# A transformer block pair on one core: the overflow blocks of the expert layer in another order on every engine

## The reference

```python
_, eidx = lax.top_k(scores + router_bias.astype(jnp.float32), TOP_K_EXPERTS)
...
def expert_block(args):
    e, toks, gs = args
    xb = t[toks]
    return swiglu(xb, w1[e], w3[e], w2[e]) * gs[:, None]
...
routed = jax.ops.segment_sum(out.reshape(rows, D), row_tok, num_segments=n_tok)
```

## Time and profile before

| what | us |
|---|---|
| median of 3 runs | 2405.52 |
| lowest and highest run | 2403.63, 2409.03 |
| the profiled execution, its own time | 2403.76 |
| its span, first to last instruction | 2402.0 |
| step 0 of the experts to the last | about 460 to 1053 |
| the three overflow blocks | about 1053 to 1098 |
| loading and adding up the rows | 1101 to 1154 |

### The profile page before, as it was taken

The page is one execution under the profiler, slowest core; times in us unless marked ns, Lnnn a source line. Parts: engine busy times, 40 slices in busy tenths (PEclk is TensorE's granted clock), DMA queues, the critical chain, the costliest instruction groups (busy, mean ns, idle before and its releaser), DMA issues.

```text
span 2402.0 us, 30744 instructions
## 1 busy us (share of the span) xinstructions
PE 2260.3 (94%) x10236; PEld 1761.8 (73%) x10236; DVE 1568.2 (65%) x2403; ACT 1198.4 (50%) x1774; POOL 237.7 (10%) x312
## 2 busy tenths in 40 slices
PE   7999999899999999992999999999999889999997
PEld 5776676778888888872666788888778557888885
DVE  7789766899999999986665643333452676433344
ACT  4433434588888888871335332233222673322333
POOL 0000000333323333320000000000020000000000
PEclk9999999999999999996999999999999899999999
DMA  8411243799999999986220222223222001322332
GB/s 332 169 62 62 88 158 125 267 367 395 381 390 401 388 387 388 378 309 282 100 77 1 79 97 96 96 96 106 97 88 97 27 14 66 114 96 96 105 102 82
DMA packets 97377, 424.09 MB, mean 177 GB/s; under 512 B 20305, under 2 KB 20561, under 8 KB 70496
## 3 DMA queue, kind: packets, MB, share of 16 engines
q1 hardware_dynamic: 77168, 386.86, 43.6%
q0 software_dynamic: 19648, 34.72, 3.8%
q10 hardware_dynamic: 432, 0.87, 0.1%
HBM read 421.81 MB, written 39.45 MB: 192 GB/s over the span
## 4 chain that ended last, share of the span: by engine, by line
PE 77%; DVE 8%; issue 5%; ACT 5%; DMA 3%; DVEq 2%; SPq 0%; POOLq 0%; POOL 0%; ACTq 0%
PE PS L298 22%; PE PS L300 21%; PE PS L299 21%; ACT wh L192 3%; PE PS L714 2%; PE PS L2006 2%; PE PS L736 2%; DMA YG<-expert_rows 1%; DVE wl L197 1%; PE PS L725 1%; DMA ada_wa<-wada 1%; PE PS L2031 1%; DVEq L1285 1%; DVE M L1282 1%; PE PS L1245 1%
## 5 line engine op out<-in xcount | busy, mean ns | idle before, releaser
L197 DVE TENSOR_TENSOR wl<-raw,wh 128x1024 fp32r<-128x1024 f32 x239 | 292.4, 1225 | 357.1 <-ACT wh L192 350.9
L298 PE MATMUL PS<-HTh,wh 128*128 128x512 f32 x1248 | 498.5, 399 | 6.3 <-ACT V L881 2.2
L300 PE MATMUL PS<-HTh,wl 128*128 128x512 f32 x1248 | 486.9, 390 | 0.0
L299 PE MATMUL PS<-HTl,wh 128*128 128x512 f32 x1248 | 486.9, 390 | 0.0
L197 DVE TENSOR_TENSOR wl<-eraw,wh 128x1024 fp32r<-128x1024 f32 x384 | 458.5, 1221 | 17.5 <-ACT wh L192 14.5
L192 ACT ACTIVATE wh<-raw 128x1024 fp32r<-128x1024 f32 x239 | 252.0, 1056 | 368.9 <-PE PS L300 344.5
L192 ACT ACTIVATE wh<-eraw 128x1024 fp32r<-128x1024 f32 x384 | 392.5, 1054 | 16.8 <-PE PS L300 14.7
L298 PEld LDWEIGHTS PS<-HTh,wh 128*128 128x128 f32 x1248 | 234.5, 188 | 72.3 <-issue 13.7
L299 PEld LDWEIGHTS PS<-HTl,wh 128*128 128x128 f32 x1248 | 234.7, 188 | 50.0 <-issue 3.4
L300 PEld LDWEIGHTS PS<-HTh,wl 128*128 128x128 f32 x1248 | 234.7, 188 | 49.6
L298 PE MATMUL PS<-wh,XTh 128*128 128x512 f32 x536 | 221.1, 413 | 2.7 <-DVE wl L2192 1.5
(11 more groups left out here) (416 smaller groups left out, 3432.2 us busy)
## 6 DMA issues: line engine op xcount, KB each, us to landing
eraw<-wstream SPq DMA_DIRECT2D x192, 1024.0 KB, 7.5
raw<-wstream SPq DMA_DIRECT2D x240, 512.0 KB, 3.3
YG<-expert_rows SPq DMA_DIRECT2D x16, 1024.0 KB, 15.8
ada_w<-wada SPq DMA_DIRECT2D x20, 512.0 KB, 5.6
eraw<-wexp SPq DMA_DIRECT2D x9, 1024.0 KB, 6.8
ada_wb<-wada SPq DMA_DIRECT2D x2, 2048.0 KB, 15.5
ada_l<-wada SPq DMA_DIRECT2D x8, 512.0 KB, 3.4
ada_g<-wada SPq DMA_DIRECT2D x2, 2048.0 KB, 10.4
```

Of the source, the lines that this page charges most:

```text
L197: nc.vector.tensor_tensor(wl[:, ci % RING, :], src, wh[:, ci % RING, :].bitcast(F32), ALU.subtract).then_inc(split_done, 1)
L298: nc.tensor.matmul(o, lh, rh, start=start, stop=False)
L299: nc.tensor.matmul(o, lh, rl, start=False, stop=False)
L300: return nc.tensor.matmul(o, ll, rh, start=False, stop=stop)
```

## The change

TensorE, ScalarE, VectorE. The rows of block p + 1 are turned ahead of chunks 2 and 3 of block p, and chunks 0 and 1 of block p + 1 go between chunks 3, the turned `HG` and 4 of block p; for block 0 they go into step 63, ahead of the down chunks of expert 63. `XTh`, `XTl`, `SG`, `HG`, `HHh`, `HHl` and bank 0 or 1 alternate by p mod 2. The four slots of `wh` and `wl` follow the new order (`more_at`). `YS` of block p is read out inside ScalarE's block p + 1 (`previous_y`), and at the end of the last block for that one.

GpSimd. Gate of p + 2 and gather of p + 3 stand behind the output copy of p; ahead of block 0's copy stand gate 1 and gather 2. There is a drain between the copy of `YIXC` and the output copy. In the last block GpSimd also waits for the gather of p + 3. SyncE waits for two more products ahead of the third pair of a block's chunks.

```diff
+            def more_at(p, c):
+
+                return c if p == 0 and c < 2 else 6 * p - 2 + c if c < 2 else 6 * p + c if c < 4 else 6 * p + 2 + c
+
+            def more_slot(p, c, i):
+
+                return (c - 2 if p == 0 and c < 2 and not isinstance(i, int) else more_at(p, c)) % RING
+
+            def more_turn(p, c, i):
+
+                at = -2 + c if p == 0 and c < 2 and not isinstance(i, int) else more_at(p, c)
+                return i * (6 * GROUP) + at
...
                 act.wait_ge(ov["xt"], i * GROUP + (p + 2))
-                if isinstance(i, int) and p == 0:
-                    act.wait_ge(chunk_used, up_end(E - 2))
-                nc.scalar.activation(XTh[:, 0, :], PS[:, 2:4, :].rearrange("p a b -> p (a b)"), ACT.Copy).then_inc(ov["xc"], 1)
+                if isinstance(i, int) and p < 2:
+                    act.wait_ge(chunk_used, up_end(E - 2 + p))
+                else:
+                    act.wait_ge(ov["used"], i * (6 * GROUP) + (6 * (p - 2) + 4 + ER))
+                nc.scalar.activation(XTh[:, p % 2, :], PS[:, 2:4, :].rearrange("p a b -> p (a b)"), ACT.Copy).then_inc(ov["xc"], 1)
...
+                nc.vector.tensor_tensor(XTl[:, p % 2, :], PS[:, 2:4, :].rearrange("p a b -> p (a b)"),
+                                        XTh[:, p % 2, :].bitcast(F32), ALU.subtract).then_inc(ov["xl"], 1)
...
+                if isinstance(i, int) and p == 0 and c < 4:
+                    act.wait_ge(chunk_used, EXPERT1 + c + 1)
+                else:
+                    act.wait_ge(ov["used"], more_turn(p, c, i) + (ER - RING + 1))
+                nc.scalar.activation(wh[:, more_slot(p, c, i), :], eraw[:, ER_PLACE[g % ER], :], ACT.Copy).then_inc(ov["high"], 1)
...
+                dve.wait_ge(ov["high"], more_turn(p, c, i) + 1)
+                nc.vector.tensor_tensor(wl[:, more_slot(p, c, i), :], eraw[:, ER_PLACE[g % ER], :],
+                                        wh[:, more_slot(p, c, i), :].bitcast(F32), ALU.subtract).then_inc(ov["split"], 1)
...
+            def more_product(pe, p, c, i=0):
+
+                pe.wait_ge(ov["split"], more_turn(p, c, i) + 1)
...
+                    if c < 4:
+                        r = slice((2 * c + kk) * P, (2 * c + kk) * P + P)
+                        mm = three_pass(PS[:, p % 2, :], XTh[:, p % 2, r], XTl[:, p % 2, r], wgh, wgl, c + kk == 0, c + kk == 4)
+                    else:
+                        r = slice((c - 4) * P, (c - 3) * P)
+                        mm = three_pass(PS[:, 6 + kk, :], HHh[:, p % 2, r], HHl[:, p % 2, r], wgh, wgl, c == 4, c == 5)
+                mm.then_inc(ov["used"], 1)
...
+            def after(eng, p, i):
+
+                return more[eng.engine] > i * GROUP + (p + 1)
+
+            def no_more(eng, p, i):
+
+                return more[eng.engine] <= i * GROUP + (p + 1)
...
+                    if n + 1 == E:
+                        with pe.If(more[pe.engine] > 0):
+                            pe.wait_ge(ov["xl"], 1)
+                            more_product(pe, 0, 0)
+                            more_product(pe, 0, 1)
...
+                    if n + 1 == E:
+                        with act.If(more[act.engine] > 0):
+                            more_high(act, 0, 0)
+                            more_high(act, 0, 1)
                     act_ht(act, n, i)
...
                     split(d0 + 1 + AHEAD, at)
                     if n + 1 == E:
                         with act.If(more[act.engine] > 0):
-                            for c in range(2):
-                                more_high(act, 0, c)
+                            more_high(act, 0, 2)
+                            more_high(act, 0, 3)
                     act_y(act, n, i)
...
+                        with dve.If(more[dve.engine] > 0):
+                            more_low(dve, 0, 0)
+                            more_low(dve, 0, 1)
                     dve_ht(dve, n, i)
...
                         with dve.If(more[dve.engine] > 0):
-                            for c in range(2):
-                                more_low(dve, 0, c)
+                            more_low(dve, 0, 2)
+                            more_low(dve, 0, 3)
...
-                        sp.wait_ge(ov["used"], i * (6 * GROUP) + (g + 2))
+                        sp.wait_ge(ov["used"], i * (6 * GROUP) + (g + (4 if c == 4 else 2)))
                         sp.dma_start(eraw[:, at:at + 2, :], wexp[e, c:c + 2].rearrange("c p n -> p c n")
                                      ).then_inc(expert_arrived[g % ER // 2], 16)
...
                 def block_(p, i):
                     y = 2 + p % 2
-                    more_gate(p + 1, i)
+                    if isinstance(i, int) and p == 0:
+                        more_gate(1, 0)
+                        more_gather(pool, 2, code_of(2, 0), 0)
                     pool.tensor_copy(YIXC[:, y:y + 1], YIX[:, bass.ds(code_of(p, i), 1)])
-                    more_gather(pool, p + 2, code_of(p + 2, i), i)
+                    pool.drain()
                     pool.wait_ge(ov["y"], i * GROUP + (p + 2))
                     pool.sem_inc(passed_pool, 1)
                     pool.indirect_dma_start(out=yrows, out_offset=bass.IndirectOffsetOnAxis(ap=YIXC[:, y:y + 1], axis=0),
...
                     pool.wait_ge(ov["rows"], i * (16 * GROUP) + 16 * (p + 3))
                     pool.sem_inc(passed_pool, 1)
+                    more_gate(p + 2, i)
+                    more_gather(pool, p + 3, code_of(p + 3, i), i)
+                    with pool.If(no_more(pool, p, i)):
+                        pool.wait_ge(ov["rows"], i * (16 * GROUP) + 16 * (p + 4))
+                        pool.sem_inc(passed_pool, 1)
```

The blocks of TensorE, ScalarE and VectorE:

```diff
+                    more_xt(pe, p + 1, i)
+                    more_product(pe, p, 2, i)
+                    more_product(pe, p, 3, i)
+                    with pe.If(after(pe, p, i)):
+                        pe.wait_ge(ov["xl"], i * GROUP + (p + 2))
+                        more_product(pe, p + 1, 0, i)
+                    pe.wait_ge(ov["hid"], i * GROUP + (p + 1))
+                    with pe.If(no_more(pe, p, i)):
+                        pe.sem_inc(ov["used"], 2)
+                    for f in range(2):
+                        mm = nc.tensor.transpose(PS[:, 4, f * P:(f + 1) * P], HG[:, p % 2, f * P:(f + 1) * P], const("ident"))
+                    mm.then_inc(ov["ht"], 1)
+                    with pe.If(after(pe, p, i)):
+                        more_product(pe, p + 1, 1, i)
+                    pe.wait_ge(ov["hl"], i * GROUP + (p + 1))
+                    pe.wait_ge(y_ready, E)
+                    pe.wait_ge(ov["y"], i * GROUP + (p + 1))
+                    more_product(pe, p, 4, i)
+                    more_product(pe, p, 5, i)
...
-                    for c in range(2, 6):
-                        more_high(act, p, c, i)
+                    more_xh(act, p + 1, i)
+                    if p or not isinstance(i, int):
+                        previous_y(p, i)
+                    with act.If(after(act, p, i)):
+                        more_high(act, p + 1, 0, i)
+                        more_high(act, p + 1, 1, i)
                     act.wait_ge(ov["used"], i * (6 * GROUP) + (6 * p + 4 + ER))
-                    nc.scalar.activation(SG[:, 0, :], PS[:, 0, 0:256], ACT.Silu).then_inc(ov["silu"], 1)
+                    nc.scalar.activation(SG[:, p % 2, :], PS[:, p % 2, 0:256], ACT.Silu).then_inc(ov["silu"], 1)
+                    with act.If(no_more(act, p, i)):
+                        act.sem_inc(ov["high"], 2)
+                    more_high(act, p, 4, i)
                     act.wait_ge(ov["ht"], i * GROUP + (p + 1))
-                    nc.scalar.activation(HHh[:, 0, :], PS[:, 4, 0:256], ACT.Copy).then_inc(ov["hc"], 1)
-                    more_xh(act, p + 1, i)
-                    with act.If(more[act.engine] > i * GROUP + (p + 1)):
-                        for c in range(2):
-                            more_high(act, p + 1, c, i)
-                    act.wait_ge(ov["used"], i * (6 * GROUP) + (6 * p + 6 + ER))
+                    nc.scalar.activation(HHh[:, p % 2, :], PS[:, 4, 0:256], ACT.Copy).then_inc(ov["hc"], 1)
+                    more_high(act, p, 5, i)
+                    with act.If(after(act, p, i)):
+                        more_high(act, p + 1, 2, i)
+                        more_high(act, p + 1, 3, i)
+                    with act.If(no_more(act, p, i)):
+                        previous_y(p + 1, i)
+
+                def previous_y(q, i):
+                    act.wait_ge(ov["used"], i * (6 * GROUP) + (6 * q + 2 + ER))
                     for s in range(2):
                         act.wait_ge(y_out[s], 16 * E // 2)
-                    act.wait_ge(ov["sent"], i * GROUP + (p + 1))
-                    nc.scalar.activation(YS[:, p % 2, :], PS[:, 6:8, :].rearrange("p a b -> p (a b)"), ACT.Copy).then_inc(ov["y"], 1)
+                    act.wait_ge(ov["sent"], i * GROUP + q)
```

(24 more changed lines are left out.)

38 lines of the change are left out of this document (5 added, 33 removed).

## The result

| | before | changed |
|---|---|---|
| median of 11 runs each | 2403.69 | 2411.03 |
| lowest and highest | 2396.15, 2409.03 | 2408.29, 2420.74 |
| the profiled execution, its own time | 2403.76 | 2408.29 |
| its span | 2402.0 | 2406.5 |

The ratio is 1.0041, with a 95% interval of 1.0028 to 1.0054: 6.7 to 13.0 us slower, 9.9 in the middle. The two medians alone are 7.3 apart, inside that interval. One execution of the changed kernel, of 4596.93, stands alone and is left out of the row of lowest and highest and of the ratio; without it the median would be 2410.85. The forecast was 2416, slower than before; the range of 2406 to 2424 holds the time.

The account below looks back on a forecast made before the run. The prediction took GpSimd seeing its last DMA land as the bound on the overflow stretch. Its steps moved that from 1098.2 to 1110.7, 12.5 us slower, so 2403.8 became 2416.3; own range 2410 to 2421, wider range 2406 to 2424.

Parts of the forecast that it names:

- Step (1): Step 63: two new products and splits stand ahead of the readout of expert 63, making it 4.7 us later.
- Step (2): Output copy 63: issued 2.0 us behind the readout, lands 5.1 later; its drain ends at 1069.9 instead of 1066.0.
- Step (3): Gather 2: issued at 1073.2, 5.2 us in flight; block 2's rows turned at 1078.4 instead of 1076.01.
- Steps (4) and (5): Block 2's rows to block 3's: 11.9 us; last block, turning to readout: 10.0 instead of 5.6, GpSimd deciding copy 2.
- Step (6): Tail: copy 2 lands, drain, then GpSimd waits for an absent block's gather; last landing 1110.7 instead of 1098.2.
- The signs: Traces expected if right, including drains of 3 to 6 us and TensorE idle 4 to 6 before block 2's turning.
- A drain doesn't wait for landings: GpSimd's drains: long ones end with landings only by chance; 4.4 us slower, 2408; chance 0.12.
- The overlap does its work: Overflow blocks: GpSimd's waits fall beside TensorE's work, gather 2 issued by 1068, idle 6.5 us filled; 2397.3; chance 0.06.
- The loads are heavier: DMA under weight loads: copy 63 lands 6.0 later, its drain lasts 4 longer, copy 0 takes 5.1; 2423; chance 0.12.

Follow-up runs that it names:

- early: tail with the first split of block 0 moved up into step 62, both products still ahead of the down products of expert 63; 2407.23, ratio 1.0020.
- tail: Changed kernel, but in the last block GpSimd neither issues nor waits for the absent block's gather, nor reads its gate; 2407.26, ratio 1.0026.
- compold: Old orders on TensorE, ScalarE and VectorE with the changed kernel's order on GpSimd; 2406.76, ratio 1.0015.
- poolold: Changed kernel's orders on TensorE, ScalarE and VectorE with the old order on GpSimd, no wait for an absent block's gather; 2412.01, ratio 1.0035.
- best4: Changed kernel with no absent gather, one product ahead in step 63, readout first, semaphore waits for drains, four XG slots, gathers four blocks ahead; 2401.04, ratio 0.9993.

## Why the prediction was right, point by point

The forecast of 12.5 us was 1.6 too much against the traces (10.9) and lies inside the interval of the ratio (6.7 to 13.0). The path was right. Two of its terms were off by 2 us each in opposite directions, so that the sum is as near as it is is in part luck.

**Step (1), readout of expert 63, 4.7 later.** Measured 6.7. The order was right, the size was not: I let the two products run at full clock. TensorE waited 2.3 for the first split, 0.3 more than I had worked out, and behind that wait the clock was 0.59 and 0.84; nine slow matmuls are 1.6 of the missing 2.0. early shows it by taking 1.5 off the wait.

**Step (2), landing of copy 63, 5.1.** It was 2.9, and this made up for step (1) by chance. I took the weight load as half done; since SyncE's third load waits for two more products and copy 63 comes 6.7 later, the load beside it (issued at 8.7, landed at 15.6) was nearly through. The drain ended at 16.15 behind the turning; I had 16.5.

**Step (3), gather 2.** Issue at 20.2 (forecast 19.8): the second gate copy with its drain took 1.2, more than I gave it. In flight for 3.8, not 5.2. Rows of block 2 1.4 later instead of 2.4; this is 1.0 of the 1.6.

**Steps (4) and (5).** Period 11.75 (11.9), turning to readout in the last block 9.85 (10.0). The new drain behind `YIXC` holds copy 2 by 0.4 (0.6): GpSimd decides, as forecast, but barely. This part I had by counting what stands in a row on each engine.

**Step (6), the tail.** From copy 2 to the last landing 7.8 (7.9). tail confirms it by itself. The way out was 2.53 (2.55 before), and no new branch cost anything near it.

**The signs.** Two of those I had named as right didn't come. The drains behind the four output copies were 2.2 to 3.0 us long, not 3 to 6, since the copies landed sooner than I had taken; each ended with its landing all the same. And TensorE was idle for 1.80 ahead of the turning of block 2, not 4 to 6: up to that point it waited 5.9 in all, but 2.32 and 1.34 of it for splits. The last DMA waited for was the gather, 4.2 behind the landing of copy 2, and everything behind the first load had the same length.

**What the sum hid.** I treated the parts as a chain. compold and poolold show +4.7 and +10.5, which is 15.2 in sum and not 10.9: GpSimd's new order costs 4.7 with the old compute order, but with the new one it is worth as much as it costs. I also let each late transfer count in full. In the table of gather 2, being late up to 16.9 costs nothing; only the part beyond counts. The 6.7 us at the readout became 3.2 at the issue of gather 2, since copy 63 landed after 2.9 and not 6.0, and 1.4 at the rows, since the gather was in flight for 3.8 and not 5.7.

**The rivals.** *A drain doesn't wait for landings* falls: compold's 6.7 and early's 6.2 end within 0.2 us of a landing. What the Trainium skill (GPSIMD Engine Reference, "Instruction dispatch") says of completion by signal doesn't describe these drains. Only the first drain of the overflow gathers, 10.4 to 12.2 us in every kernel that has it, ends with no landing that I can name. It costs nothing: without it gather 0 was issued 10 us earlier and the turning came at the same 1047.6. *The overlap does its work* falls at its own point: gather 2 was issued at 20.2 and not by 14.6 (its 1068), and best4 shows that even without any gather to wait for it wouldn't have come. *The loads are heavier* falls with 2.9 for copy 63.

## What to carry to other kernels

Before overlapping stages on the compute engines, count what each saves per block and what the first and the last pay: here 0.5 us of waiting saved ahead of the last block against 1.2 more in it, with three blocks. An unconditional prefetch at the end of a loop is on the path as soon as something waits for everything to have landed. And a transfer issued earlier beside a large load may land no earlier (four traces here); look for what is in flight before you shorten the way to its issue.
